# Attention scores and values from stacked halves, and where VectorE does the low halves

## What is computed

```
h = rms_norm(x, norm1_g)
z = h @ w_in
cb, cc, ch, q, k, v, ga, gb = jnp.split(z, IN_OFFSETS, axis=-1)
u_ext = jnp.concatenate([conv_hist, cc * ch], axis=1)
y_conv = (cb * short_conv(u_ext, conv_w)) @ w_conv_out
s = jnp.einsum('...qkgd,...skd->...kgqs', qg, k) * (HEAD_DIM ** -0.5)
p = jnp.exp(s - m)
p = p / (jnp.sum(p, axis=-1, keepdims=True) + jnp.exp(sink - m))
o = jnp.einsum('...kgqs,...skd->...qkgd', p, v)
mix = jax.nn.sigmoid(ga) * y_conv + jax.nn.sigmoid(gb) * (o @ w_attn_out)
x = x + mix @ w_o
x = x + hier_moe(rms_norm(x, norm2_g), ...)
```

## Time and profile before

| | |
|---|---|
| median of three runs | 1739.17 us (1738.9 to 1740.45) |
| the profiled execution | 1738.65 us, its span 1737.1 us |
| PE busy | 1653.6 us (95%) |
| VectorE busy | 1036.5 us (60%) |
| ScalarE busy | 834.0 us (48%) |
| GpSimd busy | 234.0 us (13%) |
| stage B, third steps of the first and last pass | 232.1 to 580.0 us from the span's start |

### The profile page before, as it was taken

The page is one execution under the profiler, slowest core; times in us unless marked ns, Lnnn a source line. Parts: engine busy times, 40 slices in busy tenths (PEclk is TensorE's granted clock), DMA queues, the critical chain, the costliest instruction groups (busy, mean ns, idle before and its releaser), DMA issues. The chain is left out here.

```text
span 1737.1 us, 26183 instructions
## 1 busy us (share of the span) xinstructions
PE 1653.6 (95%) x9527; PEld 1474.4 (85%) x9527; DVE 1036.5 (60%) x1839; ACT 834.0 (48%) x1202; POOL 234.0 (13%) x197
## 2 busy tenths in 40 slices
PE   5999999999999999999999999699999999999991
PEld 4899899999999999999999888478888888877871
DVE  5322466656556432114222576788989899888883
ACT  5000355555555430113112211378788888877773
POOL 1100000000000100000000111322322323222310
PEclk9999999999999999999999999799999999999996
DMA  6242111111111301114113711799999999999956
GB/s 161 79 125 86 40 41 46 49 36 36 36 49 48 101 25 49 49 36 158 41 44 120 255 73 72 266 379 375 379 375 372 381 370 380 373 368 367 365 206 218
DMA packets 131856, 305.30 MB, mean 176 GB/s; under 512 B 30403, under 2 KB 92079, under 8 KB 106935
## 3 DMA queue, kind: packets, MB, share of 16 engines
q1 hardware_dynamic: 115415, 267.76, 42.2%
q0 software_dynamic: 16384, 36.76, 7.3%
HBM read 282.81 MB, written 40.41 MB: 186 GB/s over the span
## 5 line engine op out<-in xcount | busy, mean ns | idle before, releaser
L1847 DVE TENSOR_TENSOR e_lo<-e_raw,e_hi 128x2048 fp32r<-128x2048 f32 x192 | 434.5, 2287 | 58.6 <-ACT e_hi L1332 34.1
L1332 ACT ACTIVATE e_hi<-e_raw 128x2048 fp32r<-128x2048 f32 x192 | 366.1, 1921 | 64.6 <-PE bank L1033 30.2
L1031 PE MATMUL bank<-e_hi,xT_hi 128*128 128x512 f32 x512 | 206.8, 404 | 6.7 <-DVE xT_lo L1852 6.7
L1127 ACT ACTIVATE w_hi<-w_raw 128x1024 fp32r<-128x1024 f32 x68 | 71.6, 1053 | 284.4 <-PE bank L704 252.8
L702 PE MATMUL bank<-h_hi,w_hi 128*128 128x344 f32 x624 | 202.8, 325 | 1.1 <-DVE h_lo L1452 1.1
L1033 PE MATMUL bank<-e_hi,xT_lo 128*128 128x512 f32 x512 | 202.5, 395 | 0.0
L1032 PE MATMUL bank<-e_lo,xT_hi 128*128 128x512 f32 x512 | 201.9, 394 | 0.0
L703 PE MATMUL bank<-h_lo,w_hi 128*128 128x344 f32 x624 | 199.9, 320 | 0.0
L704 PE MATMUL bank<-h_hi,w_lo 128*128 128x344 f32 x624 | 199.8, 320 | 0.0
L847 PE MATMUL bank<-h_hi,w_hi 128*128 128x344 f32 x576 | 197.3, 342 | 2.0 <-DVE w_lo L1433 2.0
L848 PE MATMUL bank<-h_lo,w_hi 128*128 128x344 f32 x576 | 184.8, 321 | 0.0
(11 more groups left out here) (327 smaller groups left out, 3134.6 us busy)
## 6 DMA issues: line engine op xcount, KB each, us to landing
e_raw<-in_w_e_gate_dram SPq DMA_DIRECT2D x64, 1024.0 KB
e_raw<-in_w_e_up_dram SPq DMA_DIRECT2D x64, 1024.0 KB
e_raw<-in_w_e_down_dram SPq DMA_DIRECT2D x64, 1024.0 KB
w_raw<-in_w_in_dram SPq DMA_DIRECT2D x104, 256.0 KB, 3.1
a_spill<-y_sb POOLq DMA_DIRECT2D x8, 516.0 KB, 2.9
a_raw<-a_spill SPq DMA_DIRECT2D x2, 2064.0 KB, 9.6
x_tok<-in_x_prompt_dram SPq DMA_DIRECT2D x4, 1024.0 KB, 10.7
w_raw<-in_w_attn_out_dram SPq DMA_DIRECT2D x32, 128.0 KB, 2.9
```

Source lines behind the costliest of these rows:

```text
L1031: pe.matmul(out, xT_hi[:, par, kk, :], wh, start=kk == 0, stop=False)
L1332: A.activation(e_hi[:, slot % 4, :], e_raw[slot][:, :], ACT.Copy).then_inc(e_hi_done, 1)
L1847: V.tensor_tensor(e_lo[slot][:, :], e_raw[slot][:, :], e_hi[:, slot % 4, :].bitcast(F32), ALU.subtract).then_inc(e_lo_done, 1)
```

## The change

**Scores.** The two halves of a head's queries are stacked into one operand of 128 partitions: `q_a` holds the high half of head 0 in partitions 0 to 63 and its low half in 64 to 127, `q_b` the other way round for head 1. `kk_hi` holds the keys' high half in both halves of the partitions, `kk_lo` the low half in both. So two float32r matmuls a head give all four products, where one float32 matmul of 64 rows stood.

**Values.** `vv` holds v's high and low halves side by side as columns, so that one matmul gives two results: the wanted one in one half of the output's partitions and the rest in the other. Eight matmuls replace twelve. The rest has to be moved across the partitions and added: ScalarE's `store_o` copies it to `o_rest`, and VectorE's new `add_rest` adds it to the wanted half and writes `q_sb`.

**New or moved work, by engine.** VectorE gains `queries_low` (two subtractions of 64x512) and `keys_low` (four of 64x256), each twice a pass, and `add_rest` (two of 64x512), twice a pass. They stand behind the `sinkd` that releases the exponentials, as do `split_lo` (now i = 1, 4 and 7) and `vv` (i = 2), except for `keys_low(j+1, 0)`: that stands in i = 8. The second step of the convolution moves to i = 7 and the third, with `leave(6)` and `leave(7)`, to i = 8. ScalarE gains `twin` (two copies of 64x256, twice a pass). GpSimd's `stage` becomes two calls a pass of four copies each, the first after pair 3's scores, the second after pair 7's.

**Buffers.** `w_lo` now lies where `w_raw` lies, and is written in place, so a weight block is loaded when PE has finished with the slot's last unit (`chunk_done`), no longer when its low half is made (`lo_ready`). The v units use slots 0 and 2 instead of 0 and 1, and stage C's slots are swapped. `values` in chunks 3, 5 and 7 moves from k = 2 to k = 4.

```diff
-        w_lo = at("w_lo", RING + 24576, [3, KT, P], F32R)
+        w_lo = at("w_lo", RING, [3, KT, P], F32R)
...
             def cols(slot, w, col, wait=None):
                 if wait is not None:
-                    sp.wait_ge(lo_ready, wait)
+                    sp.wait_ge(chunk_done, wait)
...
+            def stage(b, t):
+                if not isinstance(b, int):
+                    pool.wait_ge(scores_ready, b * 8 + (4 * t - 4))
+                st = slice(4 * t, 4 * t + 4)
+                pool.tensor_copy(q_a[0:64, st, :], q_sb[0:64, st, bass.ds(b * P, P)])
+                pool.tensor_copy(q_b[64:128, st, :], q_sb[64:128, st, bass.ds(b * P, P)])
...
+                pool.tensor_copy(kk_hi[0:64, 2 * t, keys], k_sb[0:64, bass.ds(t, 1), old].rearrange("p a s -> p (a s)"))
+                pool.tensor_copy(kk_hi[64:128, 2 * t + 1, keys], k_sb[64:128, bass.ds(t, 1), old].rearrange("p a s -> p (a s)")).then_inc(staged, 1)
...
-                if st == 0:
-                    pe.wait_ge(staged, b * 2 + 2)
+                if st % 4 == 0:
+                    pe.wait_ge(staged, b * 2 + (t + 1))
+                    pe.wait_ge(twin_done, b * 2 + (TWIN_FROM + t + 1))
+                    pe.wait_ge(stage_lo, b * 2 + (STAGE_FROM + t + 1))
...
-                    mm = pe.matmul(SCB[h][:, place + off:place + 256], q_stage[64 * h:64 * h + 64, st, :],
-                                   k_stage[64 * h:64 * h + 64, t, off:256], start=True, stop=True)
+                    q2, out = (q_a, q_b)[h], SCB[h][:, place + off:place + 256]
+                    pe.matmul(out, q2[:, st, :], kk_hi[:, 2 * t + h, off:256], start=True, stop=False)
+                    mm = pe.matmul(out, q2[:, st, :], kk_lo[:, 2 * t + h, off:256], start=False, stop=True)
...
-                        pe.matmul(out, vh, ph, start=kt == kts[0], stop=False)
-                        pe.matmul(out, vh, pl, start=False, stop=False)
-                        mm = pe.matmul(out, vl, ph, start=False, stop=kt == 1)
+                        v2 = vv[:, kt, t, 2 * h:2 * h + 2, :].rearrange("p a d -> p (a d)")
+                        pe.matmul(out, v2, probsT_hi[:, h, kt, :, :], start=kt == kts[0], stop=False)
+                        mm = pe.matmul(out, v2, probsT_lo[:, h, kt, :, :], start=False, stop=kt == 1)
...
+            def queries_low(b, t):
+                dve.wait_ge(staged, b * 2 + (t + 1))
+                st, now = slice(4 * t, 4 * t + 4), bass.ds(b * P, P)
+                V.tensor_tensor(q_a[64:128, st, :], q_sb[0:64, st, now], q_a[0:64, st, :].bitcast(F32), ALU.subtract)
+                V.tensor_tensor(q_b[0:64, st, :], q_sb[64:128, st, now], q_b[64:128, st, :].bitcast(F32), ALU.subtract)
...
+                for h in range(2):
+                    own, other = slice(64 * h, 64 * h + 64), slice(64 - 64 * h, 128 - 64 * h)
+                    for dst in (own, other):
+                        ins = V.tensor_tensor(kk_lo[dst, 2 * t + h, keys], k_sb[own, t, old], kk_hi[own, 2 * t + h, keys].bitcast(F32), ALU.subtract)
+                ins.then_inc(stage_lo, 1)
...
                 for i in range(9):
+                    if i == 8:
+                        step.after(V.scalar_tensor_tensor(y_sb[:, :], u_sb[:, 2:T + 2], w[2], y_sb[:, :], ALU.mult, ALU.add))
+                        leave(6)
+                        leave(7)
+                        if not last:
+                            keys_low(j + 1, 0)
...
+                    if i == 0 and not first:
+                        queries_low(j, 1)
+                    if i in (1, 4, 7):
+                        split_lo(j * 3 + (U_B + i // 3 + 1), (i // 3 + 2) % 3)
+                    if i == 2 and not first:
+                        add_rest(1, j - 1)
...
+                    if i == 3 and not first:
+                        keys_low(j, 1)
+                    if i == 5 and not last:
+                        queries_low(j + 1, 0)
+                    if i == 6:
+                        add_rest(0, j)
```

## The result

The changed kernel takes 1722.4 us in the median of five runs (1718.0 to 1726.0), against 1738.9 for the kernel before (five runs, 1737.6 to 1740.5). The ratio is 0.991, 95% interval 0.9897 to 0.9923: some 16 us faster, where 29.6 were forecast. The profiled execution took 1722.0 us, its span 1720.5; before the span was 1737.1.

What follows compares the result with a forecast made beforehand. PE's work was taken as the bound. Savings of 21.9 (passes 1 to 6), 4.75 (pass 7), 1.9 (pass 0) and 1.1 us (the ends), together 29.6, took 1738.65 to 1709.0, or 1709.5 as median; range 1702 to 1723.

Steps and rivals of the forecast that it cites:

- the wait in the passes: End of each pass with a successor: PE waits 1.1 us for VectorE's `keys_low(j+1, 0)`; a pass takes 46.1 us.
- the price of nothing for stage C's loads: Stage C: weight loads at `chunk_done` cost nothing, some 5.5 us hidden by a unit of 11.3 us on PE.
- the 0.3 us for the start of stage B: Start of stage B: `scores(0)` comes 2.1 us behind `split_lo`, everything comes 1.4 earlier, so 0.3 us is lost.
- rival 2: VectorE or GpSimd is dearer than priced: PE waits 2 to 4 us a pass, 1716 to 1730 us; chance 0.22.
- signs of being wrong: PE waits inside the pass, over 2 us or not at all before it, or at its weights in stage C.
- V's second block: Ahead of stage B: V's second block need no longer wait for its slot; 1.4 us saved.
- pass 0: Stage B's first pass: half the keys, so half the saving, 2.4 us, less half a stall: 1.9 us saved.
- passes 1 to 6: Stage B: each pass saves 4.75 us of PE's work less a wait of 1.1: 3.65 each, 21.9 us together.
- pass 7: Stage B's last pass: no `keys_low` behind it, so the full 4.75 us is saved.
- Rival 1: In the passes VectorE keeps up, PE's hand-over or the subtractions being cheaper: 36.8 us saved, 1702.5 us; chance 0.12.
- Rival 3: PE's clock falls to half after the wait before a pass, 1.6 us each; at each pass 1720.5 us; chance 0.08.
- The rule weighed in the prediction: VectorE instructions with two SBUF inputs and GpSimd ones reading SBUF exclude each other; most new subtractions can be held.

Runs made afterwards that it cites:

- e1: Changed kernel with `keys_low(j+1, 0)` moved from i = 8 to i = 7, behind `invert_sums(7)`: 1710.6 us, ratio 0.9849 to the kernel before.
- e3: Changed kernel with stage B's first `split_lo`, `queries_low(0, 0)` and `keys_low(0, 0)` placed behind the copies of V's row tiles 3, 4 and 5: 1714.1 us.
- e6: Changed kernel with the scores again as two plain float32 matmuls of 64 rows, all other engines' work kept: 1740.3 us, ratio 1.0011 to the kernel before.
- e7: Changed kernel with 12 matmuls, not 8, in a call of values, as in the kernel before: 1735.3 us, ratio 0.9986 to the kernel before.
- e2: Changed kernel with a separate place for the weights' low half in stage C, units 1 to 31, so loads wait only for `lo_ready`: 1713.0 us.
- e5: Changed kernel with the second step of the convolution moved back from i = 7 to i = 6: 1717.4 us, ratio 0.9878 to the kernel before.
- e8: Changed kernel with the weights of unit 18 issued between the two halves of `a_raw`: 1720.1 us, ratio 0.9898 to the kernel before.

## Why the prediction was half right

The sign and the place of the wait in the passes held. The sum did not: 29.6 us were forecast and 16.6 came, in the two profiled executions. **The steps that failed are the price of nothing for stage C's loads, where 6.8 us were lost, and the 0.3 us for the start of stage B, where it was 2.4.** That 1722.4 still lies in 1702 to 1723, by 0.6 us, owes something to luck: the forecast's own range was 1705 to 1716. The total falls into rival 2's band of 1716 to 1730, but not by its cause, since no wait ahead of a pass was over 1.45 us. One of the prediction's own signs of being wrong came true, waits of PE at its weights in stage C (they show as waits for `o_lo` and `a_lo`, which stand behind the weights). By its terms, in us saved:

| term | forecast | measured | where the measured comes from |
|---|---|---|---|
| V's second block | 1.4 | 1.3 | V's first matmul at 159.37 for 160.69, the wait at L795 |
| start of stage B | -0.3 | -2.4 | lead of 1.3 at V, -1.1 at chunk 0 (191.45 for 190.36) |
| pass 0 | 1.9 | 1.0 | lead -0.1 at pass 1 |
| passes 1 to 6 | 21.9 | 18.4 | first scores of pass 1 to those of pass 7: 298.97 us before, 280.55 after |
| pass 7 | 4.75 | 4.9 | rest to PE's first transpose of stage C (588.58 and 565.40), lead 23.2 |
| stage C | 0 | -6.8 | lead 16.4 behind it |

**Passes.** The mechanism was right. Two sizes were off. PE is spared 2.6 + 1.9 = 4.5 us a pass and not 4.75, almost all of it in the scores (0.33 a pair for 0.36). And `keys_low` is 1.71 us for my 1.4: I took the 0.34 from one start to the next of a 128x256 subtraction, but these rows of 64x256 take 0.43 each and do not overlap. So the chain ends 0.4 later than forecast, PE starts 0.14 behind its end, and wanted it 0.2 later: a wait of 1.41 for the 1.1. Rival 1 (VectorE keeps up) did not come true in the kernel as it stands, but e1 shows that it was one line away. Rival 2's dearer subtractions came true, but at 0.3 us a pass and not 2 to 4. Rival 3 did not occur: after idling 1.41 us PE kept the full clock, 1.00 in the whole pass.

**Start of stage B.** Here the step itself failed. I said that `scores(0)` comes 2.1 us behind `split_lo`, that "everything comes 1.4 earlier", and that 0.3 is lost. But the 1.4 was already a term of the sum, so it was counted once as a gain and once more against the loss: by my own working the loss was 0.3 + 1.4 = 1.7, and 2.4 was measured. The trace adds up: `split_lo` ended 2.1 us earlier than before (188.2 for 190.3), of which 1.3 is V's lead. Behind it stand `queries_low` 1.40 and `keys_low` 1.18, which is 2.6 us and not 2.1, and then 0.5 for PE's scores, which I left out. e3 shows all of it to be a matter of order. With VectorE idle for 2.4 us between V's tiles, the work fits in there.

**Pass 0.** I let the stall at its end be half of one, and it is 0.99 us. The rest, about 0.5 us, is not placed; the clock's fall is in both kernels.

**Stage C.** This is the largest miss. "I cost it at nothing, hidden by the unit on PE, with 5 us to spare" priced an empty queue (3 us) and one low half (1.2 us) behind the load. At unit 18 the load took 6.7 us behind `a_raw`, and behind it in VectorE's order came eight more subtractions of 1.15 us, which PE takes one by one. So the 5 us were already spent. At unit 4 the same happens with `o_lo` and without the traffic (1.5 us of the lead). From unit 16's gate on the changed kernel lost 5.3 us (176.2 for 170.9). PE's waits are 2.4 of them and the fall of the clock some 1.4 (e3, e6 and e7 lost 3.8 to 4.3 without it); the rest is not split further. I had named the place and allowed 3 us for it in the range, but not in the sum, and I did not walk it as I had walked the pass. e2 gives back 6.8 us, so the whole term is the load's later release. With e1, e2 and e3 put right, the same change is worth 40 us.

**GpSimd.** Its copies were dearer than I took them, though not twice as dear: 0.62 to 0.64 us for 512 columns where I had 0.51, and 0.40 for 256 where I had 0.26. So the group ran for 2.2 us, not 1.6, and ended at S + 3.0. The second step of the convolution was free of them (1274 and 219 ns). What they did hold were two tiny instructions, L1598 and L1599 (0.39 for 0.17), which cost 0.4 us in a place with room for it. The rule weighed in the prediction (the Trainium skill, SBUF — State Buffer, Who interferes with whom) is borne out by e5: put back beside the second group, the step takes 1.40 and 0.57 us, and the cast of `q_b` beside it 1.51 us for 0.62.

## What to carry to other kernels

When work is added to an engine that has room as a sum, ask in what order its deadlines fall. Here the consumer with the nearest deadline stood last, and one moved call was worth 9.4 us, on an engine that did the same work. When a buffer is released later, walk the one place where the queue is full or where a long row of work hangs behind the load, not the average unit. And a time gained upstream may enter the sum only once: carry the lead from event to event, as in the table, and it can't be counted twice.

## What the runs showed of the hardware

- VectorE's subtractions of 64x256, half of them into the other partitions, took 0.43 us each from start to start, and those of 64x512 0.69 to 0.70, as long as their records. A 128x512 one (`probsT_lo`) has a record of 0.69 us too and is followed after 0.60.
- A stall of 1.41 us ahead of each pass left the granted clock at 1.00. One of 4.37 us was followed by 0.50 and 0.78 in the windows from 192 to 196, and so was the 2.04 us of the kernel before by 0.50 and 0.81. At unit 18 the same place went both ways: 0.90 us and four stalls of 0.3 to 0.4 were followed by 0.72 from 790 to 795 in the changed kernel, and it fell in e1 and e5 too, while 1.45 and three of 0.40 in e8, 1.08 and four of 0.40 in e7, and 0.58 and four of 0.40 in e3 and e6 left it at 1.00. And the same wait of 1.74 us at V's first matmul was followed by 0.50 in two kernels of nine and by 1.00 in seven. So here the length of a wait of 1.4 to 1.8 us does not by itself tell whether the clock falls, and what does is open.
- A block of weights (two transfers of 256 KB) was there for ScalarE 3.8 us after its issue with nothing ahead of it in the queue (773.86 to 777.62 in e8), and 6.7 us behind 4 MB (774.64 to 781.37).
